# Forgetting attention in pairs of heads, and latent attention that multiplies unnormalised exponentials

## The reference

```
sb = (q @ k.T) * 64**-0.5 + (cum[q] - cum[k])     # causal
ob = softmax(sb) @ vb                             # 64 columns per head
```

```
s = (qn @ kn.T + qp @ kp.T) * MLA_SCALE           # causal
p = softmax(s);  o = p @ v                        # 64 columns per head
```

## Time and profile before

| | us |
|---|---|
| median of 3 runs (lowest, highest) | 2430.66 (2430.43, 2433.15) |
| span of the profiled execution | 2425.5 |
| median less span | 5.2 |
| TensorE busy | 2388.7 |
| VectorE busy | 1237.2 |
| GpSimd busy | 1000.8 |
| ScalarE busy | 952.3 |

### The profile page before, as it was taken

One profiled execution on the slowest core, in us unless ns is written; L12 is line 12 of the kernel. 1 busy time (PEld: TensorE's weight loads), 2 busy tenths in 40 slices (PEclk: granted clock), 3 DMA queues, 4 the chain that ended last, 5 costly groups with the idle time before them and its releaser, 6 DMA issues.

```text
span 2425.5 us, 29219 instructions
## 1 busy us (share of the span) xinstructions
PE 2388.7 (98%) x10762; PEld 1877.3 (77%) x10762; DVE 1237.2 (51%) x2086; ACT 952.3 (39%) x1438; POOL 1000.8 (41%) x744
## 2 busy tenths in 40 slices
PE   8999999999999999999999999999989999999999
PEld 6777668877888888857878888887556877888887
DVE  4453545334334436794456455556765334555454
ACT  3354345433322226524444222226766434222223
POOL 4323224333454445635425554544021233554443
PEclk9999999999999999999999999999999999999999
DMA  5212213421322233222223223232102421322331
GB/s 171 87 53 83 83 43 122 157 87 53 126 91 100 88 103 104 87 70 88 86 59 103 100 92 104 87 104 68 36 18 87 147 97 53 107 93 88 102 104 70
DMA packets 169703, 218.31 MB, mean 90 GB/s; under 512 B 6584, under 2 KB 143338, under 8 KB 169590
## 3 DMA queue, kind: packets, MB, share of 16 engines
q1 hardware_dynamic: 168278, 214.59, 27.2%
q10 hardware_dynamic: 1312, 2.21, 0.3%
HBM read 214.66 MB, written 2.12 MB: 89 GB/s over the span
## 4 chain that ended last, share of the span: by engine, by line
PE 91%; DVE 3%; ACT 2%; issue 1%; POOL 1%; DMA 1%; SPq 0%; DVEq 0%; ACTq 0%
PE ps_l L839 78%; PE ps_l L1096 3%; PE ps_l L988 2%; PE ps_s L1146 2%; PE ps_l L1222 1%; POOL w_lo L685 1%; PE ps_s L1205 1%; ACT w_hi L1444 1%; PE ps_s L1309 1%; PE ps_s L1324 1%; PE ps_s L1111 1%; DVE small L2752 0%; PE ps_s L839 0%; DVE arena L2235 0%; DVE a_lo L2287 0%
## 5 line engine op out<-in xcount | busy, mean ns | idle before, releaser
L685 POOL TENSOR_TENSOR w_lo<-w_raw,w_hi 128x512 fp32r<-128x512 f32 (+1 forms) x740 | 1000.6, 1384 | 1403.5 <-ACT w_hi L1444 1385.7
L839 PE MATMUL ps_l<-a_hi,w_hi 128*128 128x512 f32 x1936 | 763.6, 394 | 2.9 <-POOL w_lo L685 2.8
L839 PE MATMUL ps_l<-a_lo,w_hi 128*128 128x512 f32 x1952 | 758.4, 389 | 0.0
L839 PE MATMUL ps_l<-a_hi,w_lo 128*128 128x512 f32 x1936 | 754.1, 390 | 0.0
L1444 ACT ACTIVATE w_hi<-w_raw 128x2048 fp32r<-128x2048 f32 (+2 forms) x196 | 370.6, 1891 | 587.7 <-PE ps_l L839 579.5
L839 PEld LDWEIGHTS ps_l<-a_hi,w_hi 128*128 128x128 f32 x1936 | 363.0, 188 | 88.0 <-issue 10.8
L839 PEld LDWEIGHTS ps_l<-a_lo,w_hi 128*128 128x128 f32 x1952 | 366.0, 187 | 78.0 <-issue 3.1
L839 PEld LDWEIGHTS ps_l<-a_hi,w_lo 128*128 128x128 f32 x1936 | 362.7, 187 | 77.3
L839 PE MATMUL ps_l<-b_hi,w_hi 128*128 128x512 f32 (+1 forms) x892 | 329.4, 369 | 6.2 <-POOL w_lo L685 3.8
L839 PE MATMUL ps_l<-b_hi,w_lo 128*128 128x512 f32 (+1 forms) x892 | 326.7, 366 | 0.0
L839 PE MATMUL ps_l<-b_lo,w_hi 128*128 128x512 f32 (+1 forms) x892 | 326.7, 366 | 0.0
(11 more groups left out here) (294 smaller groups left out, 2509.1 us busy)
## 6 DMA issues: line engine op xcount, KB each, us to landing
w_raw<-in_ffn_w_up_dram SPq DMA_DIRECT2D x44, 1024.0 KB, 5.0
w_raw<-in_w_dram SPq DMA_DIRECT2D x32, 1024.0 KB, 5.2
w_raw<-in_ffn_w_down_dram SPq DMA_DIRECT2D x22, 1024.0 KB, 4.9
w_raw<-in_w_in_dram SPq DMA_DIRECT2D x20, 1024.0 KB, 5.3
w_raw<-in_xa_wkv_dram SPq DMA_DIRECT2D x16, 1024.0 KB, 5.5
w_raw<-in_w_kv_mem_dram SPq DMA_DIRECT2D x8, 1024.0 KB, 5.6
w_raw<-in_xa_wq_dram SPq DMA_DIRECT2D x8, 1024.0 KB, 5.1
w_raw<-in_xa_wo_dram SPq DMA_DIRECT2D x8, 1024.0 KB, 5.2
```

Of the source, the lines that this page charges most:

```text
L685: e.tensor_tensor(w_lo[:, b % 2, o], w_raw[:, b % 2, o], w_hi[:, b % 2, o].bitcast(F32), ALU.subtract).then_inc(w_lo_made[by], 1)
L839: ins = pe.matmul(o, *((v, w) if swap else (w, v)), start=first and n == 0, stop=last and n == 2)
```

## The change

Forgetting attention takes two heads per unit. `pair_events` replaces `attention_events` for it: lag 2, V one step after the last T, O and P two steps after. The scores of both heads are issued side by side, on the lower and the upper 64 rows, into two banks, then both masks (`masked_scores`). VectorE adds the `cum` terms head by head, takes both maxima with one instruction and scales head by head. The transposes of narrow units share a bank, of wide ones take two. V multiplies the two heads in turn, key tile by key tile, the one into partitions 0 to 63 and the other into 64 to 127 of one bank, and O and P handle all 128 partitions at once. The rows of `cum` come by one DMA for two heads, with a small one for the first unit. The fills lie in steps 0 to 18 instead of 0 to 35, the same 40.

Latent attention leaves the exponentials unnormalised: ScalarE writes them to buffers for two heads (`s_lat`) with their sums in `lat_sum`, TensorE transposes them after the exponential alone, ScalarE copies the tiles (`pt_lat`). V has the transposed tiles as stationary side and 64 value columns as moving side: ten products for a head, which give tokens on the partitions. New event P: VectorE takes the reciprocals of four sums and scales 256 columns of the evicted values into `o_lat`. New event W, for each pair of heads: TensorE transposes these four tiles back; O and Q are the high and low half of W's result. `latent_events` has lag 2, V one step after the last T, P and W two, Q three. Core of the diff:

```diff
+def pair_events(pairs, lag, extra, after, fill):
+    ev = []
+    n = pairs * TT
+    due = {}
+    for step in range(n + lag + 8):
+        if step < n:
+            p, i = divmod(step, TT)
+            if "K" in extra and step == 0:
+                ev.append(("K", 0, 0))
+            ev.append(("S", p, i))
+            if "K" in extra and p and i == 0:
+                ev.append(("K", p, 0))
+            if "K" in extra and i == 1 and p + 1 < pairs:
+                ev.append(("K", p + 1, 1))
+        for kind in "OP":
+            if (step, kind) in due:
+                ev.append((kind, due[step, kind], 0))
+        for item in fill.get(step, ()):
+            ev.append(("G", item, 0))
+        if (step, "V") in due:
+            ev.append(("V", due[step, "V"], 0))
+        if lag <= step < n + lag:
+            p, i = divmod(step - lag, TT)
+            ev.append(("T", p, i))
+            if i == TT - 1:
+                for kind, wait in zip("VOP", after):
+                    due[step + wait, kind] = p
+    return ev
...
+def latent_events(heads, lag):
+    ev = []
+    n = heads * TT
+    due = {}
+    for step in range(n + lag + 4):
+        for kind in "PQ":
+            if (step, kind) in due:
+                ev.append((kind, due[step, kind], 0))
+        if step < n:
+            ev.append(("S", *divmod(step, TT)))
+        for kind in "WO":
+            if (step, kind) in due:
+                ev.append((kind, due[step, kind], 0))
+        if lag <= step < n + lag:
+            h, i = divmod(step - lag, TT)
+            ev.append(("T", h, i))
+            if i == TT - 1:
+                due[step + 1, "V"] = due[step + 2, "P"] = h
+                if h % 2:
+                    due[step + 2, "W"] = due[step + 2, "O"] = due[step + 3, "Q"] = h // 2
+        if (step, "V") in due:
+            ev.append(("V", due[step, "V"], 0))
+    return ev
...
-    attention("fox", FOX_HEADS, 3, "v", 1, extra="K", after=(2, 2, 3), fills=(
+    attention("fox", FOX_HEADS, 2, "v", 2, extra="K", after=(1, 2, 2), pairs=True, fills=(
         ("gate_a", "w_in", 8, 256, [(0, 3080)], 2, "v", [0, 0, 1, 1], 2),
-        ("proj_a", "w_diff_out", 4, 512, [(0, 0), (0, 512)], 4, "a", [2, 2, 3, 3, 5, 6, 7, 7], 1),
+        ("proj_a", "w_diff_out", 4, 512, [(0, 0), (0, 512)], 4, "a", [2, 2, 3, 3, 3, 4, 4, 5], 1),
         ("gate_a+", "w_in", 8, 256, [(0, 3080 + c) for c in (256, 512, 768)], 2, "v",
-         [9, 9, 10, 11, 13, 13, 14, 15, 17, 17, 18, 19], 2),
+         [5, 6, 6, 7, 7, 7, 8, 8, 9, 9, 10, 10], 2),
         ("gate_b", "w_in", 8, 256, [(0, 4104 + c) for c in (0, 256, 512, 768)], 2, "v",
-         [21, 21, 22, 23, 25, 25, 26, 27, 29, 29, 30, 31, 33, 33, 34, 35], 2)))
+         [11, 11, 12, 12, 13, 13, 14, 14, 15, 15, 15, 16, 16, 17, 18, 18], 2)))
...
-        attention(f"mla{half}", 8, 3, "a", 1)
+        ev, at = latent_events(8, 2), {}
+        for kind, h, i in ev:
+            ring, who = {"S": (S, "a"), "T": (L, "a"), "V": (L, "v"), "W": (L, "v")}.get(kind, (None, ""))
+            if ring:
+                at[kind, h, i] = len(ring.who)
+                ring.who.append(who)
+            else:
+                at[kind, h, i] = at["V" if kind == "P" else "W", h, 0]
+        p.events[f"mla{half}"] = (ev, at)
...
+            def pair_values(name, vt):
+                at = plan.events[name][1]
+                def values(g, p, _):
+                    claim(pe, L, g)
+                    wait_read(pe, L, at["T", p, TT - 1] + 1)
+                    for k in range(TT):
+                        for e in (0, 1):
+                            ins = pe.matmul(bank(L, g)[64 * e:64 * e + 64, k * P:T], vt(2 * p + e, k), pt_row(e, k),
+                                            start=k == 0, stop=k == TT - 1)
+                    ins.then_inc(l_full, 1)
+                return values
...
+            def masked_scores(g, i, both):
+                n = P * (i + 1)
+                for e, (q, k) in enumerate(both):
+                    claim(pe, S, g + e)
+                    pe.matmul(bank(S, g + e)[:, 0:n], q, k[:, 0:n] if n < T else k, start=True, stop=False)
+                for e in (0, 1):
+                    pe.matmul(bank(S, g + e)[:, i * P:n], ident_bf[:, :], mask_bf[:, :], start=False, stop=True)\
+                        .then_inc(s_full, 1)
+            def fox_score(g, p, i):
...
-                attention(f"mla{half}", score,
-                          causal_values(f"mla{half}", lambda h: slice(64 * (h % 2), 64 * (h % 2) + 64),
-                                        lambda h, k: vh[:, k, h * 64:(h + 1) * 64]),
-                          turned=causal_turn(U[f"mla{half}"], lambda h, i: s_buf[:, i, :]))
+                ev, at = plan.events[f"mla{half}"]
+                for kind, h, i in ev:
+                    g = at[kind, h, i]
+                    if kind == "S":
+                        score(g, h, i)
+                    if kind == "T":
+                        claim(pe, L, g)
+                        wait_read(pe, S, at["S", h, i])
+                        for k in range(i + 1):
+                            ins = turn(bank(L, g)[:, k * P:(k + 1) * P], s_lat(h, i)[:, k * P:(k + 1) * P])
+                        ins.then_inc(l_full, 1)
+                    if kind == "V":
+                        claim(pe, L, g)
+                        wait_read(pe, L, at["T", h, TT - 1])
+                        for q in range(TT):
+                            for k in range(q + 1):
+                                ins = pe.matmul(bank(L, g)[:, 64 * q:64 * q + 64], pt_lat(h, q, k),
+                                                vh[:, k, h * 64:(h + 1) * 64], start=k == 0, stop=k == q)
+                        ins.then_inc(l_full, 1)
+                    if kind == "W":
+                        claim(pe, L, g)
+                        wait_read(pe, L, at["V", 2 * h + 1, 0])
+                        for q in range(TT):
+                            ins = turn(bank(L, g)[:, q * P:(q + 1) * P], o_lat(h)[:, q, :])
+                        ins.then_inc(l_full, 1)
             def mo_ready(k):
-                half, h = (0, 2 * k + 1) if k < 4 else (1, 2 * (k - 4) + 1)
...
                         u = TT * h + i
                         act.wait_ge(u_nm, NM[name] + u + 1)
-                        if u >= 4:
-                            wait_group(act, L, at["T", h - 1, i])
-                        act.activation(s_buf[:, i, 0:n], bank(S, g)[:, 0:n], ACT.Exp, bias=nm[:, u % 8:u % 8 + 1],
-                                       scale=qcol[:, i:i + 1], accum_out=ls[:, u % 8:u % 8 + 1]).then_inc(s_free["a"], 1)
+                        if h >= 2:
+                            wait_group(act, L, at["T", h - 2, i])
+                        if h >= 4:
+                            wait_read(act, L, at["V", h - 4, 0])
+                        l = TT * (h % 4) + i
+                        act.activation(s_lat(h, i), bank(S, g)[:, 0:n], ACT.Exp, bias=nm[:, u % 8:u % 8 + 1],
+                                       scale=qcol[:, i:i + 1], accum_out=lat_sum[:, l:l + 1]).then_inc(s_free["a"], 1)
                     if kind == "T":
-                        copy_turned(g, h, i)
+                        wait_group(act, L, g)
+                        if h >= 2:
+                            wait_group(act, L, at["V", h - 2, 0])
+                        act.activation(pt_lat(h, i), bank(L, g)[:, 0:n], ACT.Copy).then_inc(l_free["a"], 1)
                     if kind == "O":
-                        r = slice(64 * (h % 2), 64 * (h % 2) + 64)
                         wait_group(act, L, g)
-                        act.activation(A_hi[r, 4 * half + h // 2, :], bank(L, g)[r, :], ACT.Copy).then_inc(o_hi, 1)
+                        act.activation(A_hi[:, 4 * half + h, :], bank(L, g)[:, :], ACT.Copy).then_inc(o_hi, 1)
             mem_rstd(2)
             squares_and_z("mla_o", 4, 8, lambda ns: mem_parts(2, ns))
...
-                walk(name, 8, scores, lambda h, i, at=at: wait_read(dve, S, at["S", h, i]), s_buf,
-                     lambda i: P * (i + 1), half_values(name, A_hi, A_lo, 4 * half))
+                for kind, h, i in plan.events[name][0]:
+                    g = at[kind, h, i]
+                    if kind == "S":
+                        scores(g, h, i)
+                    if kind == "P":
+                        wait_read(dve, S, at["S", h, TT - 1])
+                        rl4, l = lat_sum[:, 4 * TT:5 * TT], TT * (h % 4)
+                        step(dve.reciprocal(rl4, lat_sum[:, l:l + TT]))
+                        wait_group(dve, L, g)
+                        if h >= 4:
+                            wait_group(dve, L, at["W", h // 2 - 2, 0])
+                        sync()
+                        dve.tensor_tensor(o_lat(h // 2)[:, :, 64 * (h % 2):64 * (h % 2) + 64],
+                                          bank(L, g)[:, 0:4 * 64].rearrange("p (q d) -> p q d", d=64),
```

(73 more changed lines are left out.)

147 lines of the change are left out of this document (99 added, 48 removed).

## The result

The changed kernel takes 2479.88 us (median of 4 runs, 2478.25 to 2488.57); the kernel before, on the same chip, 2430.55 (2430.15 to 2433.15). The ratio is 1.0209, interval 1.0191 to 1.0226: slower by 2.1%, 48 us more than forecast and outside the range. The profiled execution took 2488.57 us, the longest of the four, with a span of 2486.8 against 2425.5 before. So the two traces are 61.3 us apart, where the medians are 49.3 apart, and it is the 61.3 that the traces have to explain. The difference lies in which executions were profiled: of the changed kernel the longest, and of the kernel before one of the quick ones, for its median is 5.2 us above the profiled span, while in the runs recorded with their spans an execution is 1.8 to 2.4 us longer than its own.

A forecast was written before the change was run, and what follows sets the result against it. TensorE, busy 98% of the span, was taken as the bound, with hand-overs counting in the latent stage. Span 2425.5 - 23.6 (forgetting) + 25 (latent) = 2427, plus 5.2 from span to median: 2432 us, range 2417 to 2445.

The forecast's parts named there:

- Scores, transposes, breaks of fills, values run together: Forgetting stage, TensorE: savings of 11.7, 1.5, 0.7 and 9.7 us, together 23.6 us less.
- values together (9.7) or apart (1.1): Forgetting stage: a pair's value products take 2.30 us if simultaneous, saving 9.7 in all, or 4.43 one after the other, saving 1.1.
- rival B: Forgetting stage: value pairs don't run together, 8.6 us less saved, time 2441 us; chance 0.22.
- the cover of fills: Forgetting stage: at least 5.6 us of fills per pair's step hide VectorE and ScalarE work; costed at nothing.
- rival E: Forgetting stage: denser fills stall on weight pieces or ScalarE, 8 us or more, time 2440 us and up; chance 0.05.
- Hand-over rings of 7.47 and 9.11 us: Latent stage: waits between engines set a head's period, 7.47 us, or 9.11 where a pair's output comes in too.
- C: Latent stage keeps TensorE's pace: 23.6 and 7 us less, time 2400 us; chance 0.13.
- D: Latent stage: only the short ring holds, the low half not delaying the next maximum; 7 us less, 2425 us; chance 0.12.
- TensorE's own 6.0 us a head: Latent stage: TensorE's work per head, 6.0 against 6.43 now; alone it would save 7 us in 16 heads.
- the latent term: Latent stage: hand-overs make each half 66.6 us against 54.1, 12.5 more, 25 us in two halves.
- No other stage changes: All stages outside the two changed attention stages: no difference; what follows each starts the same way.
- The last guess: Whole kernel: if both stages are as said and the total isn't, some later weight load is to blame; no size given.

The follow-up runs named there:

- the part alone: Forgetting pairs alone, with the old latent stage and no lat_sum, against the kernel before: 2407.71 us, ratio 0.9906.
- the run with fillers: the kernel without the shift, plus 8 unread 128 by 128 products per latent head ahead of TensorE's waits: 2436.12 us, ratio 1.003.
- the kernel without the shift: Changed kernel with lat_sum in unused columns of the constants tensor, so no later SBUF tensor moves: 2457.36 us, ratio 1.0114 against the kernel before.

## Why the prediction was wrong

- Scores, transposes, breaks of fills, values run together: 23.6 us less. Right in mechanism and size: 22.7 in the trace and 22 in the time of the part alone. The dearest open bound, values together (9.7) or apart (1.1), was decided rightly by the row pair; rival B is refuted. The Trainium skill's rule on weight loads ("TensorE: Matmul & The Clock Gate", What overlaps and what doesn't), which spoke for B, does not hold for these products: 16 passes on two column halves took 2.31 us. Apart, they would have cost 6.2 and not the 8.6 of that rival.
- "These I cost at nothing", the cover of fills: right. TensorE is busy 144.64 of 145.60 us, so rival E falls too.
- Hand-over rings of 7.47 and 9.11 us: right, 7.54 and 9.13 while the clock is full, and the low half does stand ahead of a 128-wide maximum, so rivals C and D fall. The two waits that the text wanted to see before the values, 1.0 and over 2 us, are only partly there (0.68 and 1.11): the rest is spent earlier, where transposes wait for exponentials. The sum for the ring, 25, was about 30 by the estimate from the run with fillers; which part of it is short stays open.
- TensorE's own 6.0 us a head: right, 5.94 of work in one head and 6.18 in the next. But the 6.43 beside it in the text is the length of a head today, waits included (6.36 and 6.50 by turns); its work was already 36.48 us in six heads, 6.1. So the edit takes next to no work from TensorE, and the 7 us of its best case were all waits.
- **Failed: the latent term holds only the ring.** The forecast priced idle TensorE time as idle time alone, and took every duration at the full clock that the earlier trace rows showed with 50.07 us busy in 54.20. Here, after heads with 6.79 in 9.13, the clock fell to its lower level in every second head or so. By the same estimate that cost 27 us in the profiled run (19 in the profiled run of the kernel without the shift, 295.78 - 279.70 + 2.8). It wasn't among the rivals.
- **Failed: "No other stage changes".** The diff adds a tensor of 80 bytes, and the text gave it no price because no instruction of the other stages changes. It cost 23 us between the medians and 24.6 in the trace, half of the miss. The last guess, that a later weight load would be to blame for a wrong total, sent the reader the wrong way too: nothing waited, the products themselves were slower.

The misses together: 2432 + 24.6 + 5 (ring) + 19 to 27 (clock) is 2481 to 2489; the four runs are 2478 to 2489.

## What to carry to other kernels

Where a change makes TensorE wait inside a stage, price the wait twice: by its length, and by the chance that work around it runs at half the clock (here 30 us and 19 to 27). Where the waits can't go, try products that nobody reads: here 128 of them won 21 us. Where they can go, put each hand-over some steps further from what it waits for and look which bank the next wait wants. Compare the work itself first: where an edit takes none from the bounding engine, waits are all that it can win. Add no tensor to SBUF ahead of an operand of the main products without looking at where that operand then starts: put small ones into spare columns, as here, or fill up to 256 bytes, which was free in this kernel; other sizes than 80, 128, 256 and 512 bytes weren't tried. To read an unexplained loss, first compare the mean length of unchanged products in unchanged stages, before looking for a wait.

## What the runs showed of the hardware that was not expected

- Products with a 512-wide fp32r moving operand took 0.2270 us with A2 at its old start or 256 or 512 bytes on, 0.2333 at 80 bytes on and 0.2324 at 128. Why, and whether each of the two parts of A2 counts alike, wasn't tried.
- The mean granted clock swung within one stage, head by head: 0.97, 0.56, 0.98, 0.55, 1.00, 0.50, with no wait before values longer than 1.11 us between them. At the lower level 20 passes of 64 columns took 4.50 us instead of 2.42. In a low head TensorE is busy 10.61 of 11.01 us; behind it the clock is full again, the idle is back (6.79 of 9.13), and it falls again. So a ring bound by hand-overs is at times bound by TensorE.
- Two f32 products on different column halves by turns cost what one costs (2.31 us for 16 passes); the same 16 with the halves one behind the other took 3.86 (each to the start of the next product).
